# Three of four gate groups as seven block products, with sums of the activations made by GpSimd

## What is computed

```python
proj = einsum("bsd,dn->bsn", h, w_in)      # h: 512 x 1024
q, k, v, f, g_b, g_c, hc, gate_conv, gate_attn = split(proj)
ya = g_b * causal_conv(g_c * hc)           # 512 channels
yb = forgetting_attention(q, k, v, f)      # 8 heads of 64
merged = sigmoid(gate_conv) * (ya @ w_branch[0]) + sigmoid(gate_attn) * (yb @ w_branch[1])
x = x + rmsnorm(merged @ w_out)
x = x + rmsnorm((silu(h2 @ w_g) * (h2 @ w_u)) @ w_down)   # 2816 hidden
```

## Time and profile before

| | |
|---|---|
| runs | 1265.47, 1271.96, 1272.79 us, median 1271.96 |
| profiled execution | 1266.1 us, its span 1264.4 us |
| TensorE busy | 1255.5 us, 99% of the span |
| VectorE busy | 835.1 us, 66% |
| ScalarE busy | 616.1 us, 49% |
| GpSimd busy | 284.5 us, 22% |
| granted TensorE clock | full in all slices |
| chain that ended last | TensorE 92%, VectorE 5%, ScalarE 1%, issue 1% |

### The profile page before, as it was taken

How to read it: one execution, slowest core, us unless ns; L and a number is a source line. 1 busy time by engine, 2 the same in 40 slices (tenths; PEclk the granted TensorE clock), 3 DMA queues, 4 the chain that set the end, 5 groups by cost and what they waited for, 6 DMA issues and landing times.

```text
span 1264.4 us, 18243 instructions
## 1 busy us (share of the span) xinstructions
PE 1255.5 (99%) x7082; PEld 1068.1 (84%) x7082; DVE 835.1 (66%) x1618; ACT 616.1 (49%) x1276; POOL 284.5 (22%) x188
## 2 busy tenths in 40 slices
PE   8999999999999999999999999999999999999999
PEld 6788888888889999998888888888888888888887
DVE  5435664333579889888955647676767676677753
...
DMA packets 106408, 134.79 MB, mean 107 GB/s; under 512 B 9681, under 2 KB 73425, under 8 KB 106322
## 3 DMA queue, kind: packets, MB, share of 16 engines
...
...
## 4 chain that ended last, share of the span: by engine, by line
PE 92%; DVE 5%; ACT 1%; issue 1%; DMA 0%; POOL 0%; ACTq 0%; SPq 0%; DVEq 0%
PE ps L1070 13%; PE ps L1072 12%; PE ps L1071 12%; PE ps L1075 9%; PE ps L1077 9%; PE ps L1076 9%; PE ps L1305 4%; PE ps L1307 4%; PE ps L1308 4%; PE ps L1408 3%; DVE wlo L1837 1%; PE ps L1418 1%; PE ps L1390 1%; PE ps L1366 1%; PE ps L1367 1%; PE ps L1368 1%
## 5 line engine op out<-in xcount | busy, mean ns | idle before, releaser
L1837 DVE TENSOR_TENSOR wlo<-raw,whi 128x512 fp32r<-128x512 f32 (+1 forms) x292 | 241.5, 854 | 138.1 <-ACT whi L1471 137.2
L1471 ACT ACTIVATE whi<-raw 128x512 fp32r<-128x512 f32 (+2 forms) x336 | 213.5, 668 | 85.5 <-PE ps L1072 33.9
L1070 PE MATMUL ps<-whi,hth 128*128 128x512 f32 x464 | 189.1, 407 | 0.2 <-DVE wlo L1837 0.2
L1072 PE MATMUL ps<-wlo,hth 128*128 128x512 f32 x464 | 181.4, 391 | 0.0
L1071 PE MATMUL ps<-whi,htl 128*128 128x512 f32 x464 | 181.4, 391 | 0.0
L1075 PE MATMUL ps<-hth,whi 128*128 128x512 f32 (+1 forms) x416 | 164.6, 396 | 0.0
L1076 PE MATMUL ps<-htl,whi 128*128 128x512 f32 (+1 forms) x416 | 159.1, 382 | 0.0
L1077 PE MATMUL ps<-hth,wlo 128*128 128x512 f32 (+1 forms) x416 | 159.1, 382 | 0.0
L2353 POOL TENSOR_TENSOR wlo<-raw,whi 128x384 fp32r<-128x384 f32 (+1 forms) x44 | 49.1, 1133 | 412.7 <-ACT whi L1471 412.7
L1070 PEld LDWEIGHTS ps<-whi,hth 128*128 128x128 f32 x464 | 87.3, 188 | 20.8 <-issue 3.4
L1072 PEld LDWEIGHTS ps<-wlo,hth 128*128 128x128 f32 x464 | 87.2, 188 | 19.1
...
## 6 DMA issues: line engine op xcount, KB each, us to landing
raw<-in_w_gate_up SPq DMA_DIRECT2D x44, 512.0 KB, 4.8
raw<-in_l_w_in SPq DMA_DIRECT2D x32, 512.0 KB, 4.3
raw<-in_l_w_in SPq DMA_DIRECT2D x16, 1024.0 KB, 5.3
raw<-in_w_in SPq DMA_DIRECT2D x13, 1024.0 KB, 5.1
raw<-in_w_down SPq DMA_DIRECT2D x10, 1024.0 KB, 5.0
raw<-in_l_w_out SPq DMA_DIRECT2D x8, 1024.0 KB, 5.0
...
raw<-in_w_branch SPq DMA_DIRECT2D x8, 512.0 KB, 3.9
```

The costliest lines, as they stand in the source:

```text
L1070: e.matmul(o, ah, wh[:, cs], start=a, stop=False, skip_group_check=skip)
L1072: m = e.matmul(o, ah, wl[:, cs], start=False, stop=z, skip_group_check=skip)
L1471: return e.activation(out, in_, ACT.Copy, **how)
L1837: return e.tensor_tensor(out, src, hi_part.bitcast(F32), ALU.subtract)
```

## The change

Groups 1 to 3 (`GATED = 1`) are computed by seven block products. The activations are cut into four blocks, 256 tokens by 512 rows of k; the weights of a group into four blocks, 512 rows of k by 256 columns (conv gate or attention gate). Each of the seven products is 24 matmuls of 256 tokens (`gq`, quarters q) on a weight part and an activation block; parts 1, 2, 4 and 6 are differences of weight blocks that VectorE makes in the raw buffer (`bt`), products 1 to 4 use sums of activation blocks. Products 0, 2, 4 and 6 are chained in one PSUM bank (PJ[0]), 1 and 3 in another: behind 0, 1 and 2 ScalarE copies the bank out (`gp1`, `gp5`, `gu2`) before the next product adds to it; behind 3, 4 and 5 VectorE adds a kept copy (`bc`), and then comes the tanh. `gate_split` (step `bs`) is a part's ScalarE copy and VectorE low half, each 128x1024.

GpSimd makes the activation sums in eight operations of 128x1024 (`gf`): five behind the last convolution weights, two when the last head is written, one behind the last `gt`; their high and low parts are step `gh`, for group 1 alone. SP loads the next gate weights when part 6 (part 4 for the second half) is lowered.

In the down products the two token halves change places (banks, sums, kept copies); the sums `ds` stand behind the last gating operations `gx` and no longer ahead of them; the added PSUM copy of the block end goes to the token blocks 2 and 3; `ahead` is (4, 4) and was (3, 4).

```diff
+            if j >= GATED:
+                for n in (self.gt + 3 * j - 1, self.gt + 3 * j, self.gt + 3 * j + 1):
+                    self.h[n].pre = []
...
-            for i in range(2):
-                for m in range(2):
-                    if ("th", j, i, m) not in self.steps:
-                        finish(self.gate(j, i, m))
+            if j >= GATED:
+                self.gates(j)
+            else:
+                for i in range(2):
+                    for m in range(2):
+                        if ("th", j, i, m) not in self.steps:
+                            finish(self.gate(j, i, m))
+            if j == 0:
+                put("gf", 1)
+            if j == GATED - 1:
+                put("gf", 2)
             for m in range(2):
                 for s in range(2):
                     finish(self.unit(W.gt + 3 * j + 2, 16, 4, "br", j, m, s))
+                    if GATED - 1 <= j < 3:
+                        if (m, s) == (0, 0):
+                            self.gate_split(j + 1, 0)
+                            put("bt", j + 1, 0)
+                            if j == GATED - 1:
+                                put("gh", 0)
+                        elif (m, s) == (1, 0):
+                            self.gate_split(j + 1, 1)
+                            put("bt", j + 1, 1)
+                            if j == GATED - 1:
+                                put("gh", 1)
...
+        put("ds")
...
-        put("dc", 0)
-        put("dc", 1)
+        put("dc", 2)
+        put("dc", 3)
...
-        self.block_end(1, W.dn + 10, gen, (3, 4))
+        self.block_end(1, W.dn + 10, gen, (4, 4))
...
+    def gate_split(self, j, p):
+        if p == 0:
+            self.gate_turn = len(self.owners)
+        half = (self.gate_turn + p // 2) % 2
+        self.gate_slot[j, p] = half, p % 2
+        if p < 4:
+            self.gate_behind[j, p] = self.owners[self.gate_turn + p // 2 - 2]
+        else:
+            self.gate_behind[j, p] = ("gq", j, p - 4, 3)
+        if p % 2 or p == 6:
+            self.owners.append(("gq", j, p, 3))
+        self.put("bs", j, p)
+
+    def gates(self, j):
+        put, first = self.put, j == GATED
+
+        def product(p):
+            for q in range(4):
+                put("gq", j, p, q)
+        product(0)
+        self.gate_split(j, 2)
+        put("gp1", j)
+        put("bt", j, 2)
+        if first:
+            put("gh", 3)
+        self.gate_split(j, 3)
+        product(1)
+        put("gp5", j)
+        if first:
+            put("gh", 2)
+        self.gate_split(j, 4)
+        product(2)
+        put("gu2", j)
+        self.gate_split(j, 5)
+        put("bt", j, 3)
+        product(3)
+        put("bc", j, 0)
+        put("th", j, 1, 0)
+        self.gate_split(j, 6)
+        product(4)
+        put("bc", j, 1)
+        put("th", j, 1, 1)
+        product(5)
+        put("bc", j, 2)
+        put("th", j, 0, 0)
+        self.split(self.W.gt + 3 * j + 2, 8)
+        product(6)
+        put("th", j, 0, 1)
+
...
+        self.put("gf", 0)
...
-                    self.put("ds")
...
+        gs_hi = [gs[0][:, :, :], gs[1][:, :, :], past(pth), hth[A21_AT]]
+        gs_lo = [gs[2][:, :, :], gs[3][:, :, :], past(ptl), htl[A21_AT]]
...
+        GLEFT = [None, 0, 1, 3, 2]
+        GQ_BANK = [PJ[0], PJ[2], PJ[0], PJ[2], PJ[0], PJ[1], PJ[0]]
+        GQ_SUM = [None, 0, 1, None, 2, None, 3]
...
+        def gate_raw(j, p):
+            n = W.gt + 3 * j + (1 if p in (3, 4) else 0)
+            c = 1024 if p in (3, 5, 6) else 0
+            return n, raw[H[n].buf][:, c:c + 1024]
+
...
-        block_at = lambda p, t: ps[PJ[t] if p in (1, 3) else HI4[t] if p == 5 else HI4[2 + t]]
-        gu_part = lambda k: slice(0, 256) if k < 4 else slice(0, S)
+        block_at = lambda p, t: ps[PJ[2 + t] if p in (1, 3) else HI4[2 + t] if p == 5 else HI4[t]]
+        gu_part = lambda k: slice(256 if k < 4 else 0, S)
...
+                elif kind == "gq":
+                    j, p, q = a
+                    b, fb = GQ_BANK[p], q // 2
+                    if q == 0:
+                        if p in (0, 1, 5):
+                            claim(b)
+                        elif p == 2:
+                            pe.wait_ge(g_a, GKEPT(j, 0))
+                        elif p == 3:
+                            pe.wait_ge(g_a, GKEPT(j, 1))
+                        elif p == 4:
+                            pe.wait_ge(g_a, GKEPT(j, 2))
+                        else:
+                            pe.wait_ge(g_d, GD["bc", j, 1])
+                        pe.wait_ge(g_lo, GPART["bs", j, p])
+                        if 1 <= p <= 4:
+                            pe.wait_ge(g_lo, GPART["gh", GLEFT[p]])
+                    wh, wl = gate_place(j, p)
+                    o = ps[b][:, 256 * fb:256 * fb + 256]
+                    for kt in (2 * (q % 2), 2 * (q % 2) + 1):
+                        cs = slice(256 * kt + P * fb, 256 * kt + P * fb + P)
+                        if 1 <= p <= 4:
+                            ah, al = gs_hi[GLEFT[p]][:, kt, :], gs_lo[GLEFT[p]][:, kt, :]
+                        else:
+                            k, tok = kt + (4 if p >= 5 else 0), slice(256 if p == 6 else 0, 512 if p == 6 else 256)
+                            ah, al = hth[:, k, tok], htl[:, k, tok]
+                        e.matmul(o, wh[:, cs], ah, start=p in (0, 1, 5) and q == 0 and kt == 0, stop=False,
+                                 skip_group_check=True)
+                        e.matmul(o, wh[:, cs], al, start=False, stop=False, skip_group_check=True)
+                        m = e.matmul(o, wl[:, cs], ah, start=False, stop=kt == 3, skip_group_check=True)
+                    m.then_inc(mm, 1)
...
+                elif kind == "gh":
+                    i, = a
+                    act.wait_ge(gf_p, 8 if i % 2 else 6)
+                    copy(gs_hi[i], gs_lf[i]).then_inc(g_hi, 1)
+                elif kind == "bs":
+                    j, p = a
+                    n, place = gate_raw(j, p)
+                    if GQ_SUM[p] is None:
+                        act.wait_ge(raw_in[H[n].buf], H[n].landed)
+                    else:
+                        act.wait_ge(g_d, GD["bt", j, GQ_SUM[p]])
+                    act.wait_ge(mm, order.gate_behind[j, p])
+                    copy(gate_place(j, p)[0], place).then_inc(g_hi, 1)
+                elif kind == "gp1":
+                    j, = a
+                    act.wait_ge(mm, MM["gq", j, 0, 3])
+                    act.wait_ge(mg_d, 3 * (2 * j - 1) + 1)
+                    copy(gate_in(0, 0), two(ps[GQ_BANK[0]][:, :])).then_inc(g_a, 1)
+                elif kind == "gp5":
+                    j, = a
+                    act.wait_ge(mm, MM["gq", j, 1, 3])
+                    act.wait_ge(mg_d, 3 * (2 * j - 1) + 2)
+                    copy(gate_in(1, 1), two(ps[GQ_BANK[1]][:, :])).then_inc(g_a, 1)
+                elif kind == "gu2":
+                    j, = a
+                    act.wait_ge(mm, MM["gq", j, 2, 3])
+                    copy(gate_in(1, 0), two(ps[GQ_BANK[2]][:, :])).then_inc(g_a, 1)
+                elif kind == "th" and a[0] >= GATED:
+                    j, i, side = a
+                    if (i, side) == (0, 1):
+                        act.wait_ge(mm, MM["gq", j, 6, 3])
+                        e.activation(gate_in(0, 1), two(ps[GQ_BANK[6]][:, :]), ACT.Tanh, scale=0.5).then_inc(tanh_a, 1)
+                    else:
+                        act.wait_ge(g_d, GD["bc", j, {(1, 0): 0, (1, 1): 1, (0, 0): 2}[i, side]])
+                        e.activation(gate_in(i, side), gate_in(i, side), ACT.Tanh, scale=0.5).then_inc(tanh_a, 1)
...
+                elif kind == "bt":
+                    j, q = a
+                    b11, b12 = gate_raw(j, 0)[1], gate_raw(j, 4)[1]
+                    b21, b22 = gate_raw(j, 5)[1], gate_raw(j, 3)[1]
+                    for n in (W.gt + 3 * j, W.gt + 3 * j + 1):
+                        dve.wait_ge(raw_in[H[n].buf], H[n].landed)
+                    if q == 0:
+                        dve.wait_ge(g_lo, GPART["bs", j, 0])
+                        e.tensor_tensor(b11, b12, b11, ALU.subtract).then_inc(g_d, 1)
+                    elif q == 1:
+                        dve.wait_ge(g_lo, GPART["bs", j, 1])
+                        e.tensor_tensor(b11, b22, b11, ALU.subtract).then_inc(g_d, 1)
+                    elif q == 2:
+                        dve.wait_ge(g_d, GD["bt", j, 0])
+                        e.tensor_tensor(b12, b22, b12, ALU.subtract).then_inc(g_d, 1)
+                    else:
+                        dve.wait_ge(g_lo, GPART["bs", j, 5])
+                        e.tensor_tensor(b21, b21, b11, ALU.subtract).then_inc(g_d, 1)
+                elif kind == "bs":
+                    j, p = a
+                    n, place = gate_raw(j, p)
+                    wh, wl = gate_place(j, p)
+                    dve.wait_ge(g_hi, GPART["bs", j, p])
+                    lower(wl, place, wh).then_inc(g_lo, 1)
```

(32 more changed lines are left out.)

83 lines of the change are left out of this document (57 added, 26 removed).

## The result

The changed kernel takes 1272.5 us (median of 20 runs, 1268.5 to 1280.2), the kernel before 1266.4 us on the same chips (median of 20, 1265.4 to 1273.6); the ratio is 1.0036, 95% interval 1.002 to 1.0051. The prediction was 1264.7 with 1256 to 1272: the median lies above the range and the change has the other sign. The profiled execution after has a span of 1269.6 us, 5.2 more than before.

What follows compares the result with a forecast made beforehand. It took the gate stages as pure TensorE time, with VectorE's queue order deciding. Terms 1.65 - 2 x 2.3 - 1.4 - 0.3 + 0.3 = -4.35 gave 1261.8 or 1267.6; middle 1264.7 us, range 1256 to 1272.

Steps and rivals of the forecast that it cites:

- Attention: Attention stage: GpSimd's first five sums might hold a VectorE operation, 2.2 us on its queue if hit; taken as 0.3 slower.
- Group 1: First gate group: 18.95 us of products plus 4.45 of waits, 23.4 us, 1.65 more than before.
- The wait at product 2: Group 1: TensorE waits 3.2 us before product 2 for VectorE's low half, delayed by GpSimd.
- The two small waits of 0.65 and 0.6: Group 1 behind product 2: 0.65 us more at the end of product 2, 0.6 at product 6.
- the pace: Gate products: 0.1128 us per matmul of 256 columns, taken from the gate-up loop; 18.95 us for a group of 168.
- Groups 2 and 3: Second and third gate groups: no activation sums, no GpSimd; 19.45 us each, 2.3 less than before, twice.
- The small waits (0.25 and 0.2): Groups 2 and 3: product 2 is 0.25 us late and product 6 0.2 late.
- End of the feed-forward part: Near 590 us: TensorE's wait for a PSUM sum behind four VectorE sums goes, 1.4 us less.
- Block end: Before the transposes at 700.32: moving the added PSUM sum to the last two token blocks saves 0.3 us.
- The starting point: Whole kernel before: profiled execution 1266.1 gives 1261.8, the runs' median gives 1267.6; the middle, 1264.7, was predicted.
- the second (1269.7): Rival for the gate groups: VectorE's queue is late in every group as in group 1; +3.5 us, chance 0.18.
- the third (1273.7): Rival for groups 2 and 3: gate weights land 11.8 us after issue, so products wait; +7.6 us, chance 0.12.

Runs made afterwards that it cites:

- e1: Kernel before plus the first five GpSimd sums at their place in the changed kernel, read by nobody: 1270.9 us, ratio 1.0032 to the kernel before.
- e2: Changed kernel with its first five GpSimd sums moved to 54 us, where GpSimd is idle: 1266.9 us, ratio 1.0007 to the kernel before.
- e11: Changed kernel with the first five GpSimd sums at 54 us, activation sums standing 16 columns earlier in SBUF: 1267.4 us, single run.
- e3: Kernel before with only the four activation sums of the down products moved behind the last gating operations: 1264.4 us, ratio 0.9986.
- e4: Kernel before with only the token halves of the down products exchanged, with the block end's added sum and half products ahead as changed: 1267.4 us, ratio 1.0007.

## Why the prediction was wrong, step by step

**Attention, +0.3 against +5.9: the step that failed.** I bounded a hit by one operation "held to the end of a GpSimd one", 2.2 us on VectorE's queue, and took 0.3 since "few operations there have two SBUF inputs". Three things were wrong. The low halves of the weights that are split during the attention have two SBUF inputs, and they stand in the queue ahead of the `ptl` pieces that TensorE waits for. A held operation is not always released at the end of the sum that holds it: 5.06 us over two sums, 9.41 over four. And I had no price for what follows a wait of TensorE: 3.0 us after and 1.5 in e1, lost at the half clock. e1 shows that the sums alone do it, e2 that they cost nothing where TensorE does not wait for what they hold. The Trainium skill ("SBUF — State Buffer", SBUF: two separate sides) says that the pair of ports that VectorE and GpSimd share is a lock held for a whole instruction, and that a VectorE operation with two SBUF inputs takes it against a GpSimd operation that reads SBUF. The traces agree with the kind of operation (`wlo` 5.06 in place of 0.67, `ptl` with one SBUF input 1.14 as before). A hold that ends with the GpSimd instruction in the way would have been one sum of 2.4 us at most; the measured 9.41 went on over the three sums behind it, and the measurement decides.

**Group 1, +1.65 against +3.1.** The wait at product 2 was 3.2 by the working and is 3.21. The two small waits of 0.65 and 0.6 behind it did not come. What I left out is the clock behind the wait, 1.4 us (15 matmuls 0.213 apart in place of 0.117), and the pace, 0.95.

**Groups 2 and 3, -2.3 against -1.8 each.** The small waits (0.25 and 0.2) did not come, and the loads landed as worked out: the second 8.0 after the first was sent, by the working 7.75. The pace was mis-sized: 0.1184 in place of 0.1128 is 0.95 us on 168. I took the gate-up loop for the same kind of matmul, and by form it is; e11 shows that place alone can make a difference of this size, and the loop itself ran at 0.118 in four of the traces. My sentence that each us by which the second load is late delays product 2 as much is borne out by e2 (1.2 later, 1.1 us of wait).

**End of the feed-forward part, -1.4 against -1.5.** Right, and alone worth as much (e3: 1.5).

**Block end, -0.3 against +1.9.** I read the gap before one transpose and credited it, without following VectorE's queue of the last two blocks, where the sum went. The cover (1.36 for 0.7) was counted once, but the chain is longer in each of two blocks, by the sum and by ScalarE's square that now waits for it: 1.2 (e4). The other 0.7, a small VectorE operation held by a GpSimd low half that a later load made late, I had not looked for.

**The starting point.** I predicted the middle of 1261.8 and 1267.6, as the three runs lay 6 us apart. The lower was the common one.

**The rivals.** None of them is what happened. The time of the second (1269.7) and of the third (1273.7) came out near, but neither mechanism did it. The contention was named in the sum and not made a rival of its own.
